# Hybrid decoder step: value matmuls of a sample moved behind the block sums of the next sample, value gathers posted one turn later

## The reference

```python
gate = jnp.einsum('bshd,bnhd->bhsn', q, k_mean)          # k_mean: mean key of each block of 256
gate = jnp.where(fully_past[None, None], gate, NEG)
_, idx = lax.top_k(gate, 3)
...
s_sel = jnp.einsum('bqhd,bhqnjd->bhqnj', q_c, k_sel)     # scores against the 3 chosen blocks
s_sel = jnp.where(ok_sel, s_sel - slopes * dist_sel, NEG)
...
p = jax.nn.softmax(scores, axis=-1)                      # the chosen blocks and the own one
o = einsum(p_sel, v_sel) + einsum(p_own, v_own)
```

## Time and profile before

| | us |
| --- | --- |
| three runs | 677.87, 679.02, 682.09 |
| median | 679.02 |
| the profiled execution | 676.85 |
| its span, first to last instruction | 675.1 |
| PE busy | 581.3 (86%) |
| DVE busy | 401.8 (60%) |
| ACT busy | 254.9 (38%) |
| POOL busy | 134.2 (20%) |
| DMA | 159.29 MB, mean 236 GB/s |

### The profile page before, as it was taken

The page is one execution under the profiler, slowest core; times in us unless marked ns, Lnnn a source line. Parts: engine busy times, 40 slices in busy tenths (PEclk is TensorE's granted clock), DMA queues, the critical chain, the costliest instruction groups (busy, mean ns, idle before and its releaser), DMA issues.

```text
span 675.1 us, 10186 instructions
## 1 busy us (share of the span) xinstructions
PE 581.3 (86%) x4100; PEld 466.3 (69%) x4100; DVE 401.8 (60%) x608; ACT 254.9 (38%) x478; POOL 134.2 (20%) x205
## 2 busy tenths in 40 slices
PE   4779998797978888897679588876999999999997
PEld 2667676555554544546354577765999999999997
DVE  3425883769696969677642357536646566665441
ACT  1103221555372736452143233225433434433341
POOL 7110110375564757470000000000000000000000
PEclk9979998697979798997878889877999999999999
DMA  8999196459696978868390468663675865556700
GB/s 265 383 409 323 39 427 251 157 199 399 264 383 279 359 283 325 359 215 357 134 371 3 154 221 309 237 202 126 214 255 171 288 197 152 145 154 179 184 33 32
DMA packets 85198, 159.29 MB, mean 236 GB/s; under 512 B 2572, under 2 KB 61112, under 8 KB 81047
## 3 DMA queue, kind: packets, MB, share of 16 engines
q1 hardware_dynamic: 79328, 89.27, 40.0%
q0 software_dynamic: 5120, 67.71, 25.1%
q10 hardware_dynamic: 703, 1.67, 0.6%
HBM read 156.39 MB, written 2.72 MB: 236 GB/s over the span
## 4 chain that ended last, share of the span: by engine, by line
PE 67%; DVE 21%; DMA 7%; issue 2%; ACT 2%; SPq 1%; DVEq 0%; ACTq 0%
PE acc L1207 15%; PE acc L1302 12%; PE acc L1303 11%; PE acc L1304 11%; DVE sall L858 6%; PE chain L1386 6%; DVE prod L851 4%; PE acc L1174 3%; DMA wring<-in_w_ada 2%; DMA wring<-in_w_out 2%; DMA wring<-in_w_attn_proj 1%; DMA wring<-in_w_ffn_in 1%; PE psT L1404 1%; PE chain L1388 1%; DVE wlo L929 1%
## 5 line engine op out<-in xcount | busy, mean ns | idle before, releaser
L929 DVE TENSOR_TENSOR wlo<-wring,whi 128x1024 fp32r<-128x1024 f32 (+2 forms) x92 | 101.9, 1107 | 100.4 <-ACT whi L515 99.6
L1207 PE MATMUL acc<-hT,wring 128*128 128x264 f32 x576 | 158.4, 429 | 3.6 <-DVE hT L816 1.9
L1207 PEld LDWEIGHTS acc<-hT,wring 128*128 128x128 f32 x576 | 115.9, 209 | 34.9 <-issue 10.1
L1302 PE MATMUL acc<-xlo,whi 128*128 128x264 f32 x416 | 123.8, 298 | 13.5 <-DVE xT L1077 7.5
L515 ACT ACTIVATE whi<-wring 128x1024 fp32r<-128x1024 f32 (+2 forms) x92 | 88.0, 963 | 118.5 <-PE acc L1304 93.6
L1303 PE MATMUL acc<-xhi,wlo 128*128 128x264 f32 x416 | 121.0, 291 | 0.0
L1304 PE MATMUL acc<-xhi,whi 128*128 128x264 f32 x416 | 120.9, 291 | 0.0
L487 POOL TENSOR_TENSOR cvT<-cvT,cprod 128x256 f32<-128x256 f32 x120 | 87.6, 730 | 93.0 <-ACT cprod L515 76.9
L1302 PEld LDWEIGHTS acc<-xlo,whi 128*128 128x128 f32 x416 | 81.3, 195 | 18.2 <-DVE wlo L929 8.5
L1303 PEld LDWEIGHTS acc<-xhi,wlo 128*128 128x128 f32 x416 | 81.6, 196 | 0.1
L1304 PEld LDWEIGHTS acc<-xhi,whi 128*128 128x128 f32 x416 | 81.2, 195 | 0.0
(11 more groups left out here) (222 smaller groups left out, 669.2 us busy)
## 6 DMA issues: line engine op xcount, KB each, us to landing
wring<-in_w_ada SPq DMA_DIRECT2D x24, 1024.0 KB, 10.7
wring<-in_w_ffn_in SPq DMA_DIRECT2D x22, 1024.0 KB, 7.7
wring<-in_w_in SPq DMA_DIRECT2D x12, 1024.0 KB, 13.3
wring<-in_w_ffn_out SPq DMA_DIRECT2D x16, 704.0 KB, 5.8
wring<-in_w_out SPq DMA_DIRECT2D x4, 1024.0 KB, 13.9
wring<-in_w_in SPq DMA_DIRECT2D x6, 512.0 KB, 12.1
wring<-in_w_in SPq DMA_DIRECT2D x4, 768.0 KB, 11.8
wring<-in_w_conv_proj SPq DMA_DIRECT2D x2, 1024.0 KB, 6.0
```

Of the source, the lines that this page charges most:

```text
L929: v.tensor_tensor(wlo[:, place, 0:n, :], w, whi[:, place, 0:n, :].bitcast(F32), ALU.subtract)\
L1207: ins = mm(bank[:, 0:R], w[:, k, P * t:P * t + P], src[:, k, :], start=k == 0, stop=k == KD - 1)
L1302: mm(bank[:, 0:R], whi[:, place, k - k0, :], lo[:, k, :], start=k == 0, stop=False)
```

## The change

- PE: the value matmuls and their turn become two functions, `weigh_values(b)` and `turn_values(b)`. In turn b (from 1 on) the values of sample b - 1 are weighed directly behind the block sums of sample b, ahead of its gate, and turned behind the gate. Those of sample 7 are weighed behind the loop, ahead of the two `conv_unit`s, and turned behind these. Other moves: `spread_query` goes behind the gate matmuls; the second half of the third tile goes behind the mask; the first half of the second gate tile goes ahead of the spread sum (in turn 6 with the rows and sums that stood before it).
- ACT: the copies for the values (`values(b)`) go into the next turn, ahead of the prompt softmax; the copy of the third tile (GLU half or gate) goes behind the prompt softmax of the next turn; the sigmoid of the first gate and the sample's exponential now both stand ahead of the copy `prT`, the sigmoid first.
- POOL: the value gathers of sample b are posted in turn b, between the first and the second group of tap additions, and no longer at the end of turn b - 1. The first two (sample 0) stay ahead of the loop.
- DVE and SP are as before.

The diff, cut to its core:

```diff
             for b in range(B):
                 add_taps(b, 0)
+                if b >= 1:
+                    for c in range(CH):
+                        gather_v(b, c)
                 add_taps(b, 1)
                 gather_k(CH * b + 5)
                 add_taps(b, 2)
-                if b + 1 < B:
-                    for c in range(CH):
-                        gather_v(b + 1, c)
                 gather_k(CH * b + 6)
...
+            def values(b):
+
+                act.wait_ge(v_used, CH * (b + 1))
+                func(pvm[:, :], pv[:, :], ACT.Copy).then_inc(pvm_ready, 1)
+                act.wait_ge(pv_ready, b + 1)
+                for e in range(2):
+                    rows = slice(DH * e, DH * e + DH)
+                    func(oT[rows, :, S + b], pvT[rows, e:H:2], ACT.Copy).then_inc(o_ready, 1)
+
...
                 tap_products(b, 0)
+                if b >= 1:
+                    values(b - 1)
                 act.wait_ge(pb_ready, b + 1)
...
+                if 1 <= b <= 4:
+                    glu("ab"[1 - j], (b - 1) // 2 + 2)
+                elif b - 1 in THIRD:
+                    gate(int(THIRD[b - 1][1:]))
                 tap_products(b, 1)
...
+                if b < B - 1:
+                    gate(FIRST_GATE[b])
+                act.wait_ge(s2_ready, b + 1)
+                func(s1[:, :, :], s1[:, :, :], ACT.Exp).then_inc(e_ready, 1)
                 act.wait_ge(pt_ready, b + 1)
                 act.wait_ge(pp_ready, b)
                 func(prT[:, :], psT[:, 0:384], ACT.Copy).then_inc(pc_ready, 1)
 
-                act.wait_ge(s2_ready, b + 1)
-                func(s1[:, :, :], s1[:, :, :], ACT.Exp).then_inc(e_ready, 1)
-
-                if b < B - 1:
-                    gate(FIRST_GATE[b])
-                else:
-                    mod_rows(4)
                 tap_products(b, 2)
...
+                if b == B - 1:
+                    mod_rows(4)
+                    conv_rows()
                 act.wait_ge(pp_ready, b + 1)
...
+            def weigh_values(b):
 
                 pe.wait_ge(p_ready, 2 * b + 2)
                 for c in range(CH):
...
+                else:
+                    weigh_values(b - 1)
+
+                pe.wait_ge(gst_ready, b + 1)
+                for c in range(CH):
+                    ins = mm(gate_[:, QU * c:QU * c + QU], stepof[:, c, :], gsT[:, :], start=True, stop=True)
+                ins.then_inc(gate_ready, 1)
+                if b + 2 < B:
+                    spread_query(b + 2)
+                if b >= 1:
+                    turn_values(b - 1)
...
+            weigh_values(B - 1)
+            conv_unit(0)
+            conv_unit(1)
+            turn_values(B - 1)
             for t in range(2, KD):
                 conv_unit(t)
```

More of the change, by code:

```diff
@@ L1328, in _ @@
                     to_rows("kn1", kT, P, P)
-                if b + 2 < B:
-                    spread_query(b + 2)
+                else:
+                    weigh_values(b - 1)
                 pe.wait_ge(gst_ready, b + 1)
@@ L1345, in _ @@
                 ins.then_inc(mask_ready, 1)
+                if b - 1 in THIRD:
+                    tile(THIRD[b - 1], mix, 2, hT, k0=4)
                 pe.wait_ge(m1_ready, b + 1)
@@ L1365, in _ @@
                 ins.then_inc(pt_ready, 1)
+                if b == B - 2:
+                    to_rows("ct", u, S, TAPS - 1 + B)
+                    pe.wait_ge(ln_c, 1)
+                    sums("lnm", cvT, CT)
+                if b < B - 1:
+                    tile(f"g{first + 1}", mix, 1, hT, k1=5)
                 pe.wait_ge(es_ready, b + 1)
```

52 lines of the change are left out of this document (15 added, 37 removed).

## The result

| | before | changed |
| --- | --- | --- |
| median of 4 runs each, measured together, us | 678.72 | 652.04 |
| ratio of the times, 95% interval | | 0.9608 (0.955 to 0.9666) |
| profiled execution, its span | 676.85, 675.1 | 652.33, 650.6 |
| PE, DVE, ACT, POOL busy | 581.3, 401.8, 254.9, 134.2 | 580.1, 406.6, 272.9, 133.9 |
| granted clock of PE over the span | 0.924 | 0.921 |

The changed kernel is faster by 26.7 us. The forecast was 637 in a range of 627 to 657. Direction and range held, the size did not: of the 40.4 us that the prediction's sum gives, two thirds came. In all tables here the medians are of all runs of a kernel; the ratios leave out one run each of d2_tanh_halves (643.05), c3_late (697.34) and d4_tanh_before (1864.92), which took over 1.5% longer than the fastest of the same kernel.

A forecast was written before the change was run, and what follows sets the result against it. DVE waiting for PE's block sums, held behind the value matmuls, was taken as the bound. Gains of 29.3 (through turn 5) and 12.2 (turn 6), less 1.1 (turn 7), gave 40.4: 636.4 from 676.85; stated 637, range 627 to 657.

The forecast's parts named there:

- the rival with the drain: ACT's table loads uncovered, with the skill page's 1.38 us drain per load: turns of 29, 652 us; chance 0.05.
- What bounded the kernel before: DVE's copy of the block sums waits for PE's sum matmul behind the value matmuls: 54.3 us in eight turns; removed.
- The gate wait: DVE's gate copy would wait a new 1.0 us per turn, as the gate matmul now stands behind the values.
- The value gathers land in time: Posted at about 8 and 9.3 us of a turn, needed 17 and 19 us later; landing takes 8.1 to 17.0.
- Bytes and DVE as bounds of 25.0 and 24.6: Shortest turn: 25.0 us for the DMA engines' unchanged bytes, 24.6 for DVE's own chain of steps.
- Turn 7: Last turn: values of sample 6 ahead of its gate add 5.1 us; net loss 1.1, bounds -1 and +3.
- Turn 0: First turn: loads ahead of the exponential add 1.6 us (0 to 3.0); the next copy of the sums at 147.8.
- I expect its clock to stay up for most of a turn: PE in the loop: moved work fills gaps where it waited, so 23.8 us of work; clock above 0.95.
- The rival with 28.2 a turn and 648 us: PE's clock falls each turn as before: 27.2 us of work and about 1 of waits; chance 0.16.
- The exponential's wait of 0.3: DVE's wait per turn for ACT's score exponential behind two added table loads: 0 to 0.7, taken as 0.3 us.
- DVE's small steps: DVE's steps after the gate copy: taken as unchanged, within 18.5 us from gate copy to last reduction's end.
- Turn 6: From its copy of the sums to the next: 26.2 us instead of 38.4, a gain of 12.2.

The follow-up runs named there:

- d2_tanh_halves: Changed kernel with sigmoid written as tanh and the gate matmuls between the two halves of the values; 640.54 us, ratio 0.9377 to the kernel before.
- c3_late: Changed kernel with the value gathers posted behind the second group of tap additions instead of the first; 689.86 us, ratio 1.0127 to the kernel before.
- d4_tanh_before: Kernel before the change with sigmoid written as tanh; 678.84 us, ratio 1.0001 to the kernel before.
- c1: Changed kernel with tanh for sigmoid, gate matmuls between the halves of the values, and third tile's half ahead of the mask; 631.35 us, ratio 0.9306.
- the two edits of PE's order: Changed kernel with third tile's half ahead of the mask (644.25 us, 0.9527), or with gate matmuls between the halves of the values (644.44 us, 0.9533).
- d1_fill: Changed kernel with four unused 264-column matmuls added between the turn of the values and the mask; 655.06 us, ratio 0.9663 to the kernel before.
- e3_dense: Changed kernel with the third tile's half directly behind the gate matmuls, ahead of the mask; 644.25 us, ratio 0.9527 to the kernel before.
- c2_mixed: As c1, but with the third tile's half between the two halves of the values; 633.02 us, ratio 0.9341 to the kernel before.
- e2_split: Changed kernel with tap products and additions split 0 + 10 + 10 instead of 6 + 6 + 8; 665.02 us, ratio 0.9808 to the kernel before.
- e1_tanh: Changed kernel with each sigmoid written as tanh, sharing the exponential's table; 644.05 us, ratio 0.9501 to the kernel before.

## Why the prediction was right, and where its size was not

Direction and range held, and the first mechanism with them. But the forecast itself, turns of 25 to 27.4 us, did not come, and two of the signs that the prediction had named against itself did: the low stretches of the clock stayed, and the turns came out at 28 or more. A third, a wait of DVE above 1 for the exponential, stood in three of turns 1 to 5. The time fell inside the range because the range took in the rivals as well. That the measured 652 equals the price of the rival with the drain is chance; the rows have no such time (below).

- **What bounded the kernel before**, the wait for the block sums: right. It is gone from turns 1 to 5, and they are 2.6 us shorter each; 6.2 to 6.3 stood there, and new waits took the difference.
- **The gate wait** of 1.0 a turn: right, 0.74.
- **The value gathers land in time**: right, with landing times better than those of before. c3_late shows what it guards against.
- **Bytes and DVE as bounds of 25.0 and 24.6**: right, but seen only in c1, whose turns are 24.9 with both nearly full; the change itself did not reach them.
- **Turn 7**: a loss of 1.1 was forecast; from the copy to the end of the span it takes 330.4 instead of 329.6, a loss of 0.8. The gate copy waits 4.82 (5.1 forecast), and the last values begin 17.2 after the copy (15.7 to 17.3 forecast). DVE, then PE:

```profile
310.72 0.39 DVE L1024 TENSOR_REDUCE tiny<-s 128x8 f32<-128x128 f32 x1 [0.97 <-ACT s L515]
...
320.16 0.16 DVE L963 COPY gsT<-small 128x4 f32<-128x4 f32 x1 [0.48 <-PE small L1346]
...
325.69 0.15 DVE L970 COPY gate<-small 8x8 f32<-8x8 f32 x1 [4.82 <-PE small L1357]
```

```profile
337.40 3.60 PE L1330 MATMUL chain<-vring,pg 128*8 128x512 f32 x26
```

- **Turn 0**: the copy of turn 1 was forecast at 147.8 and came at 150.49. Of these 2.7 us, 2.2 are the later start (123.50 against 121.33), with nothing changed ahead of it; the other changed kernels start between 120.8 and 123.1, so this is a difference from run to run. The turn itself took 26.99 where 26.5 was forecast; in it the exponential waits 1.73, against the 1.6 taken.
- **"I expect its clock to stay up for most of a turn"**: this step failed. It said that filled gaps would keep the clock up and expected above 0.95; granted were 0.83 to 0.94, with 30.6 us at the lower level in five turns. The rival with 28.2 a turn and 648 us is what came, to the length: 28.3. The prediction had given it 0.16. Its parts fit less well: PE was busy 26.5 a turn and idle 1.8, where it had 27.2 and 1. And it had only PE's total in mind. The low stretches also fall on the tile half that ACT waits for, and so reach the exponential.
- **The exponential's wait of 0.3**: mis-sized. It was 2.09, 0.94, 1.83, 0 and 1.54 in turns 1 to 5, a mean of 1.28. The durations of the walk were right (7.3 against 6.9 from the GLU copy to the exponential's end); its start was 2.1 late, 1.5 of it from the lower clock (3.57 against 2.05). In turns 2 and 4, where that wait is short or none, DVE waits 1.20 and 0.76 for the GLU's sigmoid, which the prediction had at nothing.
- **The rule weighed against the change**, a drain of 1.38 us with each table load (the Trainium skill, ScalarE: Activation LUTs, What ACT_TABLE_LOAD costs): still no such time in the rows, and the trace does not agree. The load at 166.08 ends at 167.36, and the sigmoid starts at 167.37.
- **DVE's small steps**: taken at the old 1.84 us from gate copy to the next product; in turn 1 they took 2.59, from 154.16 to 156.75. This term was missing. The old turn 3, from which the 1.84 came, was a short one besides: in the old turns 1, 2, 4 and 5 the same steps took 2.2 to 2.5.
- **DVE as a whole in turn 1**: 24.6 forecast, less 0.26 at the gate, plus 2.09 at the exponential, 0.30 at the transposed maxima and 0.75 of small steps gives 27.5; measured 27.76.
- **Turn 6**: 28.15 instead of 26.2. The 3.60 for the layer norm's sums are gone, as forecast; waits of 0.97 for the exponential and 1.05 for the transposed maxima came instead.

In sum: 2.7 us by turn 1, 5 x 2.3 = 11.5 in turns 1 to 5, 2.0 in turn 6, and 0.3 less in turn 7: 15.9 between the forecast and the profiled run (636.4 and 652.33). How the 2.3 a turn divide between clock and loads can't be split exactly, since the one feeds the other. Taking away the loads gave 1.1 a turn back, each of the two edits of PE's order 1.0 and 1.1, and all three together 3.4, more than was missing, because the gate wait of the forecast went too. What makes the clock fall is open in part. PE's program moves it: with the gap ahead of the mask filled by added matmuls (d1_fill) the lower level held 14 us in turns 1 to 5 and not 31, with the tile half there (e3_dense) 24, in c1 14. But in d1_fill two turns still fell to 0.84, and the order of narrow and wide matmuls (c2_mixed) did not help, so no run here tells when it falls.

## What to carry to other kernels

When a change takes away the one large wait, the next bound is a chain of small ones across engines: walk each engine from the new start of the turn to the point where its neighbour wants the result, once with TensorE at its full clock and once at the lower one, and put the forecast between the two unless something shows that the clock stays up. An operation that cost nothing (a table load) has its price only in the place where it stands: taking two loads a turn out of the kernel before gave nothing, taking four a turn out of the changed one about 1 us a turn. And a gather that is posted in the turn before its use needs its margin counted to the last microsecond, since in c3_late the turns with late gathers also had the lower clock, and the loss grew over the first turns.

## What the runs showed of the hardware

- The lower clock (1.2 instead of 2.4 GHz) comes also where PE hardly waits. In turn 5 of the changed kernel, 10.2 us at the lower clock, PE was busy 28.26 of 29.50 us, and of its waits the timeline has only the two below. The low stretch is one piece: in the window ahead of them PE is busy 9.62 of 10.00 us at a granted clock of 0.50.

```profile
267.50:277.50 10.00, 9.62 (x29) 7.64 (x30) 8.08 (x14) 5.88 (x14) 2.87 (x4) 0.50 0.93 354
...
268.86 0.80 PE L1366 MATMUL small<-alib,ident 128*128 128x128 f32 x2 [0.38 <-DVE pen L990]
...
289.73 0.39 PE L1346 MATMUL small<-quad,sall 128*128 128x4 f32 x2 [0.86 <-DVE sall L862]
```

- DVE's smallest steps get longer beside POOL's work. The 8x64 `SCALAR_TENSOR_TENSOR` (L977) took 0.20 in turn 0, with POOL idle, and 0.61 at 154.95, beside the additions that run from 150.42 to 155.49; the 8x8 `TENSOR_SCALAR` (L988) 0.16 and, beside the post of the gather at 155.64, 0.41. In c3_late, where the gather is posted late in the turn, the row of L988 in turn 3 is back at 0.16; in e2_split, with no additions there and the post over, both are back at 0.20 and 0.16 in every turn. The Trainium skill (SBUF — State Buffer, SBUF: two separate sides) says that DVE and GpSimd share a port pair that one of them holds for a whole instruction while the other waits, where DVE's instruction has two SBUF inputs and GpSimd's reads SBUF, or where DVE's runs in a two-port mode. The row of L977, which has two inputs, agrees with that as far as it goes: it is longer by 0.41, less than one addition of POOL (5.07 / 6 = 0.85). L988 has one input and is longer by 0.25; no run here shows in which mode it ran.
- The DMA engines sustained 396 GB/s at a share of 1.00 over 124 us in c1_all.
- Exponential and tanh need no table load between them; exponential and sigmoid do (8 loads are left of 36 in e1_tanh; each takes 1.28 us).
